# Two layers' w_out product and first query group taken one token tile at a time

## The reference, cut to what matters

```python
def second_block(x, ...):
    for l in range(2):
        x = x + token_mixer(rms_norm_2(x, norm_mix[l]), ...)     # ends in: merged @ w_out
        x = x + peer_ffn(rms_norm_2(x, norm_ffn[l]), peer_query[l], peer_sub_keys[l], peer_down[l], peer_up[l])

def chunk(xc):                                 # peer_ffn, for each 128 tokens
    q = (xc @ w_query).reshape(128, 8, 2, 128)
    s = einsum('thpk,pnk->thpn', q, sub_keys)
    sv, si = top_k(s, 16)                      # 16 best of 128 keys, twice per head
    cand = sv[:, :, 0, :, None] + sv[:, :, 1, None, :]
    top_s, sel = top_k(cand, 16)               # 16 best of 256 pairs: the experts
    g = softmax(top_s)
    u, vv = expert_down[eidx], expert_up[eidx]
    act = gelu(einsum('td,thkd->thk', xc, u))
    return einsum('thk,thkd->td', g * act, vv)
```

## Time and profile before

| | |
|---|---|
| median of 3 executions | 2240.69 us (2240.04 to 2241.07) |
| the profiled execution's own time | 2241.91 us |
| its span | 2240.1 us |
| PE, DVE, ACT, POOL busy | 89%, 72%, 51%, 39% |
| bytes by indirect DMA | 536.9 MB of 707 MB |
| chain that ended last: PE, DMA, POOL, DVE, issue, ACT | 41%, 25%, 11%, 9%, 8%, 6% |

### The profile page before, as it was taken

How to read it: one execution, slowest core, us unless ns; L and a number is a source line. 1 busy time by engine, 2 the same in 40 slices (tenths; PEclk the granted TensorE clock), 3 DMA queues, 4 the chain that set the end, 5 groups by cost and what they waited for, 6 DMA issues and landing times.

```text
span 2240.1 us, 29611 instructions
## 1 busy us (share of the span) xinstructions
PE 1990.3 (89%) x9760; PEld 1302.1 (58%) x9798; DVE 1609.4 (72%) x3230; ACT 1144.5 (51%) x2534; POOL 874.5 (39%) x557
## 2 busy tenths in 40 slices
PE   9999999999999898977777788999899887778877
PEld 8999899998889644422222223889644432222222
DVE  4566777777787877776777765787887776777774
ACT  4455555545554655454454545565655444444443
POOL 0120000000230355566667663040355566666664
PEclk9999999999999999999999999999999999999999
DMA  7544465665636999999999997736899999999998
GB/s 247 172 132 142 148 184 180 185 189 157 219 119 219 381 421 421 421 421 421 421 418 422 420 421 302 233 116 222 334 421 421 421 421 421 422 422 411 422 421 338
DMA packets 120772, 707.23 MB, mean 316 GB/s; under 512 B 13664, under 2 KB 13920, under 8 KB 55008
## 3 DMA queue, kind: packets, MB, share of 16 engines
q0 software_dynamic: 73728, 536.90, 57.8%
q1 hardware_dynamic: 43488, 157.63, 22.4%
q10 hardware_dynamic: 3456, 11.40, 1.5%
HBM read 704.84 MB, written 1.05 MB: 315 GB/s over the span
## 4 chain that ended last, share of the span: by engine, by line
PE 41%; DMA 25%; POOL 11%; DVE 9%; issue 8%; ACT 6%; POOLq 0%; SPq 0%; DVEq 0%; ACTq 0%
DMA work<-in_experts,expert_idx 24%; PE ps L548 11%; POOL work L1098 10%; PE ps L549 10%; PE ps L550 10%; PE ps L1315 6%; DVE work L2166 2%; DVE weights_lo L533 2%; PE ps L687 1%; ACT L1616 1%; ACT L1667 1%; DMA weights<-in_wstream 1%; ACT arena L1672 1%; DVE work L2143 1%; PE ps L713 1%
## 5 line engine op out<-in xcount | busy, mean ns | idle before, releaser
L1315 PE MATMUL ps<-work,arena 128*128 128x512 f32 x2040 | 989.9, 617 | 216.1 <-ACT arena L1672 212.4
L1098 POOL DMA_INDIRECT work<-in_experts,expert_idx x512 | 790.2, 1543 | 621.2 <-PE ps L1315 291.3
L1315 PEld LDWEIGHTS ps<-work,arena 128*128 128x128 f32 x2040 | 359.0, 191 | 821.0 <-ACT arena L1672 516.2
L2166 DVE CUSTOM_DVE_ANT_0 work<-h_norm,work 128x1024 f32<-128x1024 f32 x480 | 588.1, 1225 | 334.5 <-DMA work<-in_experts,expert_idx 320.2
L1667 ACT ACTIVATE small<-small 128x1 f32<-128x1 f32 x512 | 150.2, 293 | 609.1 <-DVE small L2166 588.0
L533 DVE TENSOR_TENSOR weights_lo<-weights,weights_hi 128x1024 fp32r<-128x1024 f32 x280 | 349.8, 1255 | 152.8 <-ACT weights_hi L528 152.1
L548 PE MATMUL ps<-feat_hi,weights_hi 128*128 128x256 f32 x1528 | 445.3, 291 | 7.6 <-DVE weights_lo L533 5.8
L528 ACT ACTIVATE weights_hi<-weights 128x1024 fp32r<-128x1024 f32 x280 | 295.0, 1056 | 286.0 <-PE ps L550 232.6
L549 PE MATMUL ps<-feat_lo,weights_hi 128*128 128x256 f32 x1528 | 432.8, 283 | 0.0
L550 PE MATMUL ps<-feat_hi,weights_lo 128*128 128x256 f32 x1528 | 432.7, 283 | 0.0
L548 PEld LDWEIGHTS ps<-feat_hi,weights_hi 128*128 128x128 f32 x1528 | 293.3, 192 | 18.1 <-issue 9.3
(11 more groups left out here) (250 smaller groups left out, 1912.1 us busy)
## 6 DMA issues: line engine op xcount, KB each, us to landing
weights<-in_wstream SPq DMA_DIRECT2D x280, 512.0 KB, 4.2
work<-in_experts,expert_idx POOLq DMA_INDIRECT x512
arena<-in_wstream SPq DMA_DIRECT2D x12, 512.0 KB, 6.0
arena<-in_na_bias ACTq DMA_DIRECT2D x6, 512.0 KB, 5.3
params<-in_wstream SPq DMA_DIRECT2D x6, 512.0 KB, 5.9
arena<-in_bias ACTq DMA_DIRECT2D x5, 512.0 KB, 4.6
params<-in_par ACTq DMA_DIRECT2D x2, 576.0 KB, 5.3
params<-in_par ACTq DMA_DIRECT2D x1, 1024.0 KB, 6.7
```

The lines of the kernel that those rows point to most:

```text
L1098: nc.gpsimd.indirect_dma_start(ring[:, r, :], None, experts, bass.IndirectOffsetOnAxis(ap=EIDX[:, b, c * RING + r:c * RING + r + 1], axis= ...
L1315: ins = nc.tensor.matmul(bank(2 * t + h), DIAG[:, r, :], ring[:, r, D + h * 512:D + (h + 1) * 512], start=False, stop=False)
L2166: nc.vector.tensor_tensor_reduce(ring[:, r, 0:D], HN[:, t, :], ring[:, r, 0:D], 1.0, 0.0, ALU.mult, ALU.add, hd[:, r:r + 1]).then_inc(dots ...
```

## The change

In both layers:

- w0 to w3 stay as they were. w4 to w7 are multiplied with tile 0 first (`wo_tile`); tile 1 of w4 follows w7, tile 1 of w5 lies around the transposes of the first query group, tiles 1 of w6 and w7 follow the first key scores. Additions, transposes, high and low parts of groups 2 and 3 are made per tile.
- The first query group is computed per tile with tokens as rows (`query0`) and transposed (`query0_turned`), with its first weights packed to suit. Tile 1 of it comes after the picking.
- w4, w5 and w6's split parts go to spare places in `work`, so they and the three halves behind wait for older halves. POOL's eighth gather waits until w6 is done with, since its ring slot lies over that place.
- ACT splits w3 to w7, q0 and q1 before the first transposed part. DVE has a new order, in which the addition of group 1 follows the low parts of w6 and w7.
- The index write L2103 no longer waits for the squares. The squares, now made after the tile 1 query and the high part of q3, go to other memory. The count of `HN` parts is six per layer, and e8 waits for the sixth.

The diff, cut to what the text speaks of (eight leading spaces are taken off):

```diff
+with nc.sbuf_tensor("work_rounded", [P, 16392], F32R) as work_rounded:
+    SPARE = [work_rounded[:, a:a + 2 * HW] for a in (0, 8200, 14344)]
...
+    local = (n - L_HALF) % L_HALVES - 2 * LG_WO - 4
+    return local if n >= L_HALF and 0 <= local < SLOTS else None
...
+    return WH[:, n % SLOTS, :] if spare(n) is None else SPARE[spare(n)][:, 0:HW]
...
+    return WL[:, n % SLOTS, :] if spare(n) is None else SPARE[spare(n)][:, HW:2 * HW]
...
-    if n >= SLOTS:
-        act.wait_ge(half_done, base + n - SLOTS + 1)
-    nc.scalar.activation(WH[:, n % SLOTS, :], raw(n), ACT.Copy).then_inc(w_hi, 1)
+    if n >= SLOTS and spare(n) is None:
+        act.wait_ge(half_done, base + n - (2 * SLOTS if behind_spare(n) else SLOTS) + 1)
+    nc.scalar.activation(high(n), raw(n), ACT.Copy).then_inc(w_hi, 1)
...
-    pe.wait_ge(nm.hn, 4 * l + g + 1)
+HN_TURNS, HI_TURNS = WO + 2, 7
...
+    return (1, 2, 3 + 2 * t, 4 + 2 * t)[g]
...
+def turned_pe(pe, nm, l, g, tiles=range(TT)):
...
+    pe.wait_ge(nm.hn, HN_TURNS * l + hn_turn(g, tiles[0]))
...
-        for t in range(TT):
+        for t in tiles:
...
+def wo_tile(pe, n, t, b, at, chunks=range(HC)):
...
+    h = WO_ORDER[n][1]
+    w = split_pe(pe, L_HALF + 2 * LG_WO + n, at)
...
+        ins = product(ps[:, b * 512 + t * GC:b * 512 + (t + 1) * GC], kept(c, t * P, P), cols(w, i * GC, GC), c == 0, c == KC - 1)
+    return ins
...
-                sp.wait_ge(n_peer.hn, 4 * l + -(-min(gains_end, D) // GC))
+                sp.wait_ge(n_peer.hn, HN_TURNS * l + hn_turn(-(-min(gains_end, D) // GC) - 1))
...
+            if r == RING - 1:
+                wait_alone(pool, half_done, l * L_HALVES + L_HALF + 2 * LG_WO + 7, pool_passed)
...
-        wo_pe(pe, (lproj_taken, l * N2 + L_PROJ + L_GATE), G_LAYER + LG_WO, l, at, turned=n_peer)
+        taken0 = WO + (WO + 1) * l
+        for n in range(4):
+            wo_both(pe, (lproj_taken, l * N2 + L_PROJ + L_GATE), G_LAYER + LG_WO, n, l * BR + BR, at)
+        pe.wait_ge(wo_taken, taken0 + 1)
+        wo_tile(pe, 4, 0, 6, at)
+        turned_pe(pe, n_peer, l, 0)
+        wo_tile(pe, 5, 0, 6, at).then_inc(tile0_done, 1)
+        turned_pe(pe, n_peer, l, 1)
+        wo_tile(pe, 6, 0, 5, at).then_inc(tile0_done, 1)
+        turned_pe(pe, n_peer, l, 2, (0,))
+        wo_tile(pe, 7, 0, 5, at).then_inc(tile0_done, 1)
+        wo_tile(pe, 4, 1, 6, at).then_inc(half_done, 1)
+        turned_pe(pe, n_peer, l, 3, (0,))
...
+        def query0(t, b):
...
+            for c in range(KC):
+                if c % HC == 0:
+                    w = split_pe(pe, L_HALF + 2 * LG_PQ + c // HC, at)
+                if c % 2 == 0:
+                    pe.wait_ge(n_peer.hT, HI_TURNS * l + (1 if c == 0 else c // 2 + 1 + 3 * t))
+                ins = product(ps[:, b * 512:b * 512 + GC], feat(c, t * P, P), cols(w, c % HC * GC, GC), c == 0, c == KC - 1)
+                if t and c % HC == HC - 1:
+                    ins.then_inc(half_done, 1)
             return ins
...
+        def query0_turned(t, step):
...
+            pe.wait_ge(first_query, step)
+            for part in range(2):
+                ins = nc.tensor.transpose(ps[:, 5 * 512 + S + part * P:5 * 512 + S + (part + 1) * P], pqT[:, 4 + t, part * P:(part + 1) * P], ident)
+            ins.then_inc(tile0_done, 1)
...
-        pe.wait_ge(n_peer.hT, l * 4 + 2)
-        parts = [split_pe(pe, L_HALF + 2 * LG_PQ, at)]
-        first_part(0, range(HC))
-        turned_pe(pe, n_peer, l, 3)
-        parts.append(split_pe(pe, L_HALF + 2 * LG_PQ + 1, at))
-        first_part(1, range(HC))
-        pe.wait_ge(n_peer.hT, l * 4 + 3)
-        for part in range(2):
-            first_part(part, range(4, 6))
-        pe.wait_ge(n_peer.hT, l * 4 + 4)
-        for part in range(2):
-            first_part(part, range(6, 8)).then_inc(half_done, 1)
-        pe.wait_ge(first_query, l + 1)
+        query0(0, 7).then_inc(tile0_done, 1)
+        wo_tile(pe, 5, 1, 6, at, range(2))
+        query0_turned(0, l * 3 + 1)
+        wo_tile(pe, 5, 1, 6, at, range(2, HC)).then_inc(half_done, 1)
+        pe.wait_ge(first_query, l * 3 + 2)
         key_score(4, 0, 0, 0).then_inc(first_scored, 1)
-        pe.wait_ge(lproj_taken, l * N2 + L_PROJ + L_GATE + 1)
         key_score(5, 0, 0, 1).then_inc(first_scored, 1)
-        for part in range(2):
-            ins = key_score(3, part, 1, part)
-        ins.then_inc(sc_done, 1)
+        wo_tile(pe, 6, 1, 7, at).then_inc(half_done, 1)
+        wo_tile(pe, 7, 1, 7, at).then_inc(half_done, 1)
+        turned_pe(pe, n_peer, l, 2, (1,))
+        turned_pe(pe, n_peer, l, 3, (1,))
+        query0(1, 6)
+        query0_turned(1, l * 3 + 3)
...
+                pe.wait_ge(lproj_taken, l * N2 + L_PROJ + L_GATE + 1)
+                for part in range(2):
+                    ins = key_score(3, part, 1, part)
+                ins.then_inc(sc_done, 1)
...
-        for n in range(2 * WO - 2):
+        for n in range(2 * WO - 1):
...
-        for b in range(4):
-            if b in (0, 2):
-                act.wait_ge(half_done, wo_halves + 2 * WO - 1 + b // 2)
-            act.wait_ge(n_peer.xp, 4 * l + b + 1)
-            nc.scalar.activation(two(FH, b), bank(b), ACT.Copy).then_inc(n_peer.hi, 1)
-            if b == 1:
-                split_hi(act, L_HALF + 2 * LG_PQ + 1, at)
...
+        def turned_act(b, turn, tiles):
...
+            act.wait_ge(n_peer.xp, HN_TURNS * l + turn)
+            nc.scalar.activation(tile_pair(FH, b, tiles), tile_bank(b, tiles), ACT.Copy).then_inc(n_peer.hi, 1)
...
+        def query0_act(t):
...
+            act.wait_ge(*((half_done, at.halves + L_HALF + 2 * LG_PQ + 2) if t else (tile0_done, l * 6 + 4)))
+            nc.scalar.activation(pqT[:, 4 + t, :], bank(6 if t else 7)[:, 0:GC], ACT.Copy).then_inc(first_query, 1)
...
+        def query0_turned_act(t):
...
+            act.wait_ge(tile0_done, l * 6 + 5 + t)
+            nc.scalar.activation(pqT[:, 0:2, t * P:(t + 1) * P], bank(5)[:, S:2 * S].rearrange("p (c n) -> p c n", n=P),
+                                 ACT.Copy).then_inc(lproj_taken if t else first_query, 1)
+        turned_act(0, 1, (0, TT))
+        act.wait_ge(tile0_done, l * 6 + 2)
+        turned_act(1, 2, (0, 1))
+        act.wait_ge(tile0_done, l * 6 + 3)
+        turned_act(2, 3, (0, 1))
+        turned_act(3, 4, (0, 1))
+        query0_act(0)
+        query0_turned_act(0)
+        act.wait_ge(half_done, wo_halves + 7)
+        turned_act(1, 2, (1, TT))
+        act.wait_ge(half_done, wo_halves + 8)
+        turned_act(2, 5, (1, TT))
         split_hi(act, L_HALF + 2 * LG_PQ + 2, at)
+        turned_act(3, 6, (1, TT))
...
-        take_first(0)
-        take_first(1)
+        query0_act(1)
         hi_query(SLOTS)
+        query0_turned_act(1)
+        act.wait_ge(x_ready, l * 3 + 2 * TT + 1)
+        for t in range(TT):
+            ins = nc.scalar.activation((DIAG.rearrange("p r n -> p (r n)") if t else SC[:, 1:5, :, :].rearrange("p a s n -> p (a s n)")), X[:, t, :], ACT.Square, accum_out=ssq[:, t:t + 1])
+        ins.then_inc(n_peer.sq, 1)
+        hi_query(SLOTS + 1)
+        act.wait_ge(n_peer.var, l + 1)
+        nc.scalar.activation(std, ssq, ACT.Sqrt).then_inc(n_peer.std, 1)
...
-        hi_query(SLOTS + 1)
-        act.wait_ge(x_ready, l * 3 + 2 * TT + 1)
-        for t in range(TT):
-            ins = nc.scalar.activation(Y[:, t, :], X[:, t, :], ACT.Square, accum_out=ssq[:, t:t + 1])
-        ins.then_inc(n_peer.sq, 1)
-        act.wait_ge(n_peer.var, l + 1)
-        nc.scalar.activation(std, ssq, ACT.Sqrt).then_inc(n_peer.std, 1)
...
-        for g in range(WO):
-            if g < WO - 1:
-                los(LG_WO + g)
-            else:
-                lower(0)
-                lower(1)
-                split_lo(dve, L_HALF + 2 * LG_PQ + 1, at)
-            dve.wait_ge(half_done, at.halves + L_HALF + 2 * LG_WO + wo_done(g))
-            dst = X[:, :, g * GC:(g + 1) * GC]
-            ins = nc.vector.tensor_tensor(dst, dst, bank(6 + g % 2 if g < WO - 1 else 5).rearrange("p (t n) -> p t n", t=TT), ALU.add)
-            if g < WO - 1:
-                ins.then_inc(wo_taken, 1)
-                dve.wait_ge(wo_taken, l * (WO - 1) + WO + g + 1)
-            else:
...
-                dve.wait_ge(x_ready, l * 3 + 2 * TT + 1)
...
-        lower(2)
-        lower(3)
-        split_lo(dve, L_HALF + 2 * LG_PQ + 2, at)
...
+        def added(g, b, tiles, ready, nth):
+            dve.wait_ge(*ready)
+            n = tiles[1] - tiles[0]
+            dst = X[:, tiles[0]:tiles[1], g * GC:(g + 1) * GC]
+            src = bank(b).rearrange("p (t n) -> p t n", t=TT)[:, tiles[0]:tiles[1], :]
+            last = g == WO - 1 and tiles[1] == TT
+            nc.vector.tensor_tensor(dst, dst, src, ALU.add).then_inc(x_ready if last else wo_taken, 1)
+            dve.wait_ge(*((x_ready, l * 3 + 2 * TT + 1) if last else (wo_taken, WO + (WO + 1) * l + nth)))
+            nc.vector.tensor_tensor(HN[:, tiles[0]:tiles[1], g * GC:(g + 1) * GC], dst,
```

(60 more changed lines are left out.)

50 lines of the change are left out of this document (21 added, 29 removed).

## The result

The change costs 31.4 us: median 2271.73 us (2267.99 to 2273.07, 4 runs) against 2240.36 us of the kernel before in the same comparison (2239.51 to 2241.07), ratio 1.0137, 95% interval 1.012 to 1.0155. The forecast was 2254.2 us, slower, with 2238 to 2261 as its range: the sign is right, the loss is more than twice as large. The profiled execution after has a span of 2269.0 us; the one before, 2240.1.

A forecast was written before the change was run, and what follows sets the result against it. The prediction took the DMA, full during the gathers, as the bound. Late 13th gathers (5.3 and 6.5 us) plus 1.7 us of clock gave 13.5 us on 2241.91, 2255.4; the median, 1.2 lower, 2254.2; range 2238 to 2261.

The forecast's parts named there:

- the path to the indexes: Layer 0, up to DVE's picking: PE's saving and its new waits cancel; second index at 736.2, 1.3 us earlier.
- PE's first wait: Before group 1's transposes, PE stands 3.8 us for DVE's addition, now behind the low part of w7.
- the second wait: Ahead of w7's tile 0, PE stands 3.4 us because ACT takes q1's high part before the first transposed part.
- the 6 us that PE saves: Ahead of the first index, w4 to w7 need only tile 0, taking about 6 us of PE work out.
- POOL's wait for w6: Before the eighth gather: costs nothing, since w6's tile 1 ends at about 733.2, ahead of that gather.
- I take 5.6: 744.0: Load of q3, layer 0: issued at 738.4 behind e8, taken to land 5.6 us later, at 744.0.
- the upper bound of 9: Load of q3 behind e8: time to landing put between 4.4 and 9 us.
- let the dots absorb 0.7 us: Layer 0, behind the mean square: DVE's earlier 0.69 us wait for the exponential absorbs part; supply shifts 8.3 us.
- 1.7 us for the clock: PE after its new waits: one clock fall counted over both layers, 1.7 us; bound 0 to 3.4.
- the spare time of 3.0 and 2.8 us: At the 13th gather, layers 0 and 1: delay that the eight gathers in flight were taken to cover.
- under the longer delay: Loads e8, q3, q4, q5 moved into the full DMA stretch: about 2 us a layer, hidden by the supply delay.
- The "worse" rival: q3 takes 8.3 to 9 us and PE's clock falls more often: 3 us more per layer, 2260; chance 0.15.

The follow-up runs named there:

- E3: Kernel after, with DVE adding group 1 before w6's and w7's low parts, ACT's first transposed part before w7, q0 and q1, root table later; 2258.8 us.
- E5: Kernel after, with POOL issuing the second gather and all behind it only once ACT has made the high part of q3; 2259.7 us, ratio 1.0078.
- E2: Kernel after, with the squares, mean square and root taken ahead of the high and low parts of q3 on ACT and DVE; 2269.3 us.
- E6: Kernel before, with seven idle additions on DVE, some 3 us, ahead of the gates; 2242.3 us, ratio 1.001.
- E8: Kernel after, with e8 issued behind q6 and the edits of E2 and E3 together; 2254.7 us, ratio 1.0068.
- E9: Kernel after with e8 behind q6, E3's edit, squares right behind the last transposed part, mean square before q3's low part, q5's after first dots; 2239.4 us.

## Why the prediction was right and wrong

*Right: the path to the indexes.* Forecast 733.5 and 736.2, measured 733.28 and 735.86. PE's first wait was 4.19 us (3.8 forecast). The second was shorter (0.80 us in place of 3.4), and yet the key scores came at 731.48, where the forecast had 731.8: PE reached the second wait late, since its work ran at a lower clock, 0.88 and 0.78 of full in the two stretches from 715 to 725, behind the first wait. A fall there was harmless, as forecast. E3 shows that these waits used up the 6 us that PE saves. In layer 1 the clock fell ahead of the key scores too (0.50 from 1580 to 1585 us, behind a wait of 2.96 us), but the second index was only 14.0 us late with 15.6 us carried over from layer 0. POOL's wait for w6 cost nothing: the eighth gather was issued at 744.32, 0.30 us behind the seventh.

*Wrong, the largest: "I take 5.6: 744.0" for the landing of q3.* It took 11.5 us, beyond the upper bound of 9. The bound came from the row of a lone half among full gathers (8.3 us in the earlier trace rows), and e8 stood ahead of q3 at the same third of the rate. The reason given for the low value, "the first gathers are only starting", was wrong: the second to eighth were issued from 736.85 to 744.32, the second ahead of q3. In E5, where they were not, it took 5.6. So the mean square was 14.2 us late, not 9.0.

*Wrong: what lies behind the mean square.* The forecast had the list of instructions unchanged and let the dots absorb 0.7 us. But q4 and q5 had become late loads as well, and DVE needs their low parts ahead of the first dot (it waited 1.09 us at q5's, and in E2 1.82). PE's clock adds to it: it stood at 0.50, the lower level of 1.2 GHz, through 750 to 755, behind PE's wait of 7.12 us. From the mean square to the ninth gather there were 15.4 us before and 17.8 after, in layer 1 14.3 and 18.5. The sum had 1.7 us for the clock, for one fall ahead of the key scores. How the 2.4 and 4.2 us divide between loads and clock was not tried.

*Wrong: the spare time of 3.0 and 2.8 us.* That the 13th gather decides was right. It was issued 15.75 us late and landed 15.5 us late, so the gathers in flight hid 0.3 us. The hole had used them up: the ninth was issued 16.65 us late and landed 12.3 us late, the tenth to 12th 13.6 us late, and behind them the DMA had no reserve. It was short once more just there, 0.90 and 311 GB/s from 785 to 790 us, with no load beside the gathers. The one of the two queues that moved anything in these five us:

```profile
q0 software_dynamic: 208, 1.56, 90.3%
```

So the loads that had moved took nothing from this stretch; their bytes were through before the hole, and the forecast's "under the longer delay" holds. Even for a delay of 3 us the figure was too large (E6: 1.7 and 1.8). It let a gather's bytes flow 1.7 us after the issue; the ninth gather, alone on the DMA, took 6.3 us from issue to landing (770.78 to 777.10), 3.8 more than its 2.49 us of bytes.

Together, in layer 0, where the forecast had 5.3 us for the 13th gather and 15.5 were measured: 5.2 us of the miss are q3's landing (the mean square), 2.3 what lies between it and the 13th gather's issue, 2.7 the spare time.

*The "worse" rival* had the right side and stopped short: it gave q3 8.3 to 9 us and came to 2260.

## What to carry to other kernels

Before work is moved behind a first DMA burst, ask which loads it will issue late, and charge each of them by the packets it must share the engines with: here 3.76 us in place of 1.25, and with such loads on the gates' path the kernel is slower even with early indexes (E3: index 5.8 us earlier than before, time 18 us longer). An order of instructions that waits for a load has to be undone at every place (E2, E8), since the next low part in line waits for the next load. And the gain of an earlier start is bounded by the idle time it removes less the transfers that it leaves to the full stretch: E9 did everything as meant and came out level.
